# When a pick's factor is computed, and how many gather operations a double tile gets

## What is computed

```
def chunk(args):
    xc, ec, gc = args
    u = u_emb[ec]
    a = jax.nn.gelu(jnp.einsum('nd,nkd->nk', xc, u))
    return jnp.einsum('nk,nkd->nd', gc * a, v_emb[ec])
```

## Time and profile before

| | us |
|---|---|
| median of 3 runs | 4573.24 |
| lowest and highest | 4567.98, 4573.95 |
| the profiled execution | 4565.19 |
| its span | 4563.4 |
| TensorE busy (matmul) | 4388.7 |
| VectorE busy | 2760.2 |
| ScalarE busy | 1736.6 |

### The profile page before, as it was taken

One profiled execution on the slowest core, in us unless ns is written; L12 is line 12 of the kernel. 1 busy time (PEld: TensorE's weight loads), 2 busy tenths in 40 slices (PEclk: granted clock), 3 DMA queues, 4 the chain that ended last, 5 costly groups with the idle time before them and its releaser, 6 DMA issues. The chain is left out here.

```text
span 4563.4 us, 62015 instructions
## 1 busy us (share of the span) xinstructions
PE 4388.7 (96%) x21945; PEld 3670.3 (80%) x21945; DVE 2760.2 (60%) x4570; ACT 1736.6 (38%) x2923; POOL 797.8 (17%) x783
## 2 busy tenths in 40 slices
PE   8999999999999999999999998899999899999898
PEld 7888888888888887888888886787767788888787
DVE  5436556454344445555444288654779788777776
ACT  3323634332232235344332243442238444433333
POOL 0000000000000000000000000010677544444442
PEclk9999999999999999999999998999999999999999
DMA  3222220222222222211222221031224888888886
GB/s 136 92 102 92 92 75 37 74 95 98 101 93 92 102 86 90 105 43 47 93 101 93 100 87 65 19 129 56 93 102 184 311 323 334 320 312 319 309 307 253
DMA packets 93608, 634.50 MB, mean 139 GB/s; under 512 B 13344, under 2 KB 13728, under 8 KB 22752
## 3 DMA queue, kind: packets, MB, share of 16 engines
q1 hardware_dynamic: 58464, 412.95, 24.7%
q0 software_dynamic: 33792, 193.75, 11.2%
q10 hardware_dynamic: 1152, 25.17, 1.3%
HBM read 604.55 MB, written 27.26 MB: 138 GB/s over the span
## 5 line engine op out<-in xcount | busy, mean ns | idle before, releaser
L193 PE MATMUL PB<-XH,WH 128*128 128x512 f32 (+1 forms) x3288 | 1256.1, 382 | 41.6 <-DVE WL L3336 19.1
L195 PE MATMUL PB<-XH,WL 128*128 128x512 f32 (+1 forms) x3288 | 1234.6, 375 | 0.0
L194 PE MATMUL PB<-XL,WH 128*128 128x512 f32 (+1 forms) x3288 | 1233.9, 375 | 0.0
L174 DVE TENSOR_TENSOR WL<-RAW,WH 128x1024 fp32r<-128x1024 f32 x520 | 624.5, 1242 | 499.2 <-ACT WH L166 459.9
L193 PEld LDWEIGHTS PB<-XH,WH 128*128 128x128 f32 x3288 | 620.9, 189 | 160.0 <-DVE WL L3336 29.7
L195 PEld LDWEIGHTS PB<-XH,WL 128*128 128x128 f32 x3288 | 620.0, 189 | 100.5
L194 PEld LDWEIGHTS PB<-XL,WH 128*128 128x128 f32 x3288 | 621.8, 189 | 97.8 <-issue 1.9
L166 ACT ACTIVATE WH<-RAW 128x1024 fp32r<-128x1024 f32 x504 | 504.4, 1049 | 510.1 <-PE PB L195 481.9
L254 POOL TENSOR_TENSOR SQ<-SQ 128x512 f32<-128x512 f32 x49 | 72.5, 1480 | 2566.5 <-ACT SQ L236 2544.5
L193 PE MATMUL PB<-WH,WGH 128*128 128x512 f32 x768 | 307.7, 401 | 52.0 <-DVE WGL L3352 52.0
L3336 DVE TENSOR_TENSOR WL<-RAW,WH 128x1024 fp32r<-128x1024 f32 x220 | 269.4, 1224 | 126.4 <-ACT WH L3268 125.7
(11 more groups left out here) (441 smaller groups left out, 7153.8 us busy)
## 6 DMA issues: line engine op xcount, KB each, us to landing
RAW<-weights SPq DMA_DIRECT2D x381, 1024.0 KB, 4.8
gate_matrix<-STG ACTq DMA_DIRECT2D x4, 4096.0 KB, 12.1
GM<-gate_matrix POOLq DMA_DIRECT2D x128, 128.0 KB, 4.4
RAW<-weights SPq DMA_DIRECT2D x12, 512.0 KB, 3.8
gate_matrix<-STG ACTq DMA_DIRECT2D x3, 2048.0 KB, 7.2
GM<-gate_matrix POOLq DMA_DIRECT2D x128, 48.0 KB, 4.5
UV<-rows,IDX POOLq DMA_INDIRECT x160, 8.4
X<-x SPq DMA_DIRECT2D x4, 512.0 KB, 8.1
```

The source lines that it names most:

```text
L174: c.nc.vector.tensor_tensor(c.WL[p][:, cols], c.RAW[p][:, cols], c.WH[p][:, cols].bitcast(F32), ALU.subtract).then_inc(c.sem("w_split"), 1)
L193: c.nc.tensor.matmul(out, wh, xh, start=start, stop=False)
L194: c.nc.tensor.matmul(out, wh, xl, start=False, stop=False)
L195: return c.nc.tensor.matmul(out, wl, xh, start=False, stop=stop)
```

## The change

In `act_experts` a factor whose sum is not in the same step is no longer computed at the end of its step but in the next one, behind `high(x + 1, 0)`. A factor whose sum is in the same step stays at the end of the step. In `round_plan` a double tile has a room of 4 and no longer 5; a single one keeps 3. VectorE's, TensorE's and GpSimd's code is the same, but VectorE's order of dots and sums follows `round_plan`.

```diff
@@ round_plan
-    room = [0 if x + 1 == len(PLAN) else 5 if len(tile) == 2 else 3 for x, tile in enumerate(PLAN)]
+    room = [0 if x + 1 == len(PLAN) else 4 if len(tile) == 2 else 3 for x, tile in enumerate(PLAN)]
@@ act_experts
+    def pick_gains(x, summed):
+
+        for what, r in ROUND_PLAN[x]:
+            if what == "dot" and (("sum", r) in ROUND_PLAN[x]) == summed:
+                pick_gain(r)
...
         if more:
             high(x + 1, 0)
+        if x:
+            pick_gains(x - 1, False)
         if len(tile) == 1:
...
-        for what, r in ROUND_PLAN[x]:
-            if what == "dot":
-                pick_gain(r)
+        pick_gains(x, True)
```

## The result

The changed kernel takes 4490.42 us (median of 4 runs, 4485.33 to 4497.99), the kernel before beside it 4570.61 (4 runs, 4566.79 to 4573.95). The ratio is 0.9826, with a 95% interval of 0.9809 to 0.9843: 80 us or 1.7% faster. Forecast were 4525 with a range from 4502 to 4560. The profiled execution took 4491.90 us around a span of 4490.1, 73.3 us less than that of before.

The account below looks back on a forecast made before the run. TensorE, busy 908.2 of the loop's 980 us, was taken as the bound, waiting 71.1 us for VectorE. Without VectorE's 108 us of stalls, 48 us were to go: median 4573 - 48 = 4525 us, range 4502 to 4560.

Parts of the forecast that it names:

- The bound and the stalls: Expert loop: moving the factor removes 108 us of VectorE stalls, leaving it about 880 us, below TensorE's 908, which then paces.
- AG's thin cover: Gelu behind the moved factor: cover 0.1 us thin, 0 to 0.3 us on each of 94 single tiles; 10 us taken.
- I expect the waits for UV to stay about where they are, 40 to 70 us: VectorE's waits for gathered rows: fewer short-lead dots, but vanished stalls had also given rows time to land; 56.6 us before.
- The sum: Expert loop: TensorE becomes the bound; of its 71 us of waits a gain of 48 is taken, between 42 and 53.
- the best stretch of before: Old kernel's window 3774 to 3824, 48.44 us busy in 50; the whole loop at that rate gains 42 us.
- 3 to 5 us: TensorE's clock in the loop: fewer gaps bring its mean nearer 1.00, counted within the 48 us gain.
- The lower end of the range, 4502: Lower end of the 8 in 10 range: a gain near everything that TensorE waits, plus clock.
- (B), leads: Rival, chance 0.18: gathers' short leads decide, new row waits of 45 us against 108 saved; gain perhaps 20, 4553 us.
- (C), DMA full at 313 GB/s: Rival, chance 0.12: DMA engines already full, landing times grow by what is saved; within 5 us, 4570.
- (D), long landings: Rival, chance 0.05: earlier weight loads run beside gathers, long landings cost 60 us against 48 saved; slower, 4585 us.
- faster by more: Chance 0.87 that the whole kernel gets faster by more than about 9 us, 0.2% of its time.
- A: The forecast itself, chance 0.65: VectorE's stalls go and TensorE paces the loop; 4510 to 4538 us.

Follow-up runs that it names:

- order_only: The kernel after with a double tile's room back at 5, so only the factor is moved behind the rounding; 4509.95 us, ratio 0.9853 against the kernel before.
- gather_first_before: The kernel before, with GpSimd issuing a group's gathers ahead of its two gate-matrix loads; 4532.26 us, ratio 0.9904.
- both 4488: The kernel after with a room of 5 and the gathers issued ahead of the gate-matrix loads; 4488.40 us, ratio 0.9813 against the kernel before.
- room_only: The kernel before with a double tile's room of 4 instead of 5, the factor staying where it was; 4569.92 us, ratio 0.9985.
- a fill in each step: The kernel after with one VectorE fill of an unused 128x1024 tile ahead of each step's first WL; 4570.29 us, ratio 0.9998 against the kernel before.
- six fills: The kernel after with six such VectorE fills in a row in each of 17 double tiles; 4628.66 us, ratio 1.0130 against the kernel before.

## Why the prediction was wrong, step by step

*The bound and the stalls: right.* VectorE's regular stalls behind the factor are gone (105.3 us behind dots and sums, 7.1 now; 108 were counted), TensorE paces the loop, ScalarE's wait for PRODG fell from 337.4 to 137.7 us and its wait for TensorE ahead of the rounding grew from 19.9 to 95.9. The forecast that VectorE's waits for WH fall below 30 us was wrong, they are 83.6; the total was a bad sign to name, since it fills again at the second half of the tile when TensorE and the weights set the pace.

*AG's thin cover: harmless.* WG waited 0.9 us for AG in the whole loop, and I had put 10 us there.

*"I expect the waits for UV to stay about where they are, 40 to 70 us": wrong for the whole change, right for the order alone.* They are 19.6 us with both parts, 53.1 with the order alone. It takes both parts: the room alone leaves 47.1 us. With the order in place the room is worth 12 to 20 us. I had counted the leads (17 against 10) and then let the vanished stalls cancel them. They did not: from that WG to the dot, the dot's own wait aside, it is 13.1 us in the mean before and after. And where a lead stayed short, the rows came sooner. Round 101 has seven instructions and 7.1 us of work between WG and dot in either plan; its gather and its dot before, then after:

```profile
4163.20 1.62 POOL L3445 DMA_INDIRECT UV<-rows,IDX  x1 [0.30 <-issue]
4172.74 1.23 DVE L3319 SCALAR_TENSOR_TENSOR PRODG<-UV,XG 128x1024 f32<-128x1024 f32 x1 [4.22 <-DMA UV<-rows,IDX]
...
4133.41 1.00 POOL L3450 DMA_INDIRECT UV<-rows,IDX  x1 [0.30 <-issue]
4139.31 1.23 DVE L3324 SCALAR_TENSOR_TENSOR PRODG<-UV,XG 128x1024 f32<-128x1024 f32 x1
```

Before, the rows were there 9.5 us after the issue began, now within 5.9. Rounds 76 and 111 are alike, and in `order_only` these three don't wait either. What shortened these landings no run shows.

*The sum: the failed step.* It took what it called the best stretch of before as the pattern and left 23 to 27 us of TensorE's waits, where 17 are left; that term was 44 and measured 54. And it counted "3 to 5 us" for the clock, while TensorE's busy time fell by 21.2. Together these are 27 us of the 75 in the loop. The stretch still held all of the stalls, and it was no bound but a point on the way. It was not even the best; that one, in the kernel before, has 49.08 us of work in 50, part of it at the lower clock:

```profile
4024.00:4074.00 50.00, 49.08 (x246) 43.32 (x244) 40.29 (x51) 20.98 (x42) 21.59 (x21) 0.98 0.81 307
```

What TensorE needs was the bound: 2208 matmuls of 352 columns and 2304 of 512, at 0.161 and 0.229 us from start to start when the clock is full, are an estimated 883 us, 25 less than the 908 that I took for its work. A look at TensorE's rows behind its gaps would have shown it: in the kernel before, ten gaps have a start at half pace behind them, which costs 16 us beside the gaps (the excess over 0.161 and 0.229 us); in the kernel after one has, 1.4 us. That is 15 of the 21 us.

*The lower end of the range, 4502, "a gain near everything that TensorE waits, plus clock": wrong by its own words.* All of 71 and the 5 for the clock would have been 4497, still above the measured 4490: the clock's share had no bound of its own.

*The rivals.* (B), leads, is not what happened, but half of it was true: `gather_first_before` shows that leads alone were worth 42 us. (C), DMA full at 313 GB/s, is refuted: the loop now runs at 339 GB/s. The share of the DMA engines is 0.90, and up to 0.93 in the kernel with gathers first. (D), long landings, did not come: waits for rows fell. The chance of "faster by more" was added up wrong by a little: A, B and a quarter of C are 0.86, not 0.87.

What stays open: how far the gains of order and leads overlap in detail. The four corners are measured (none 4574, leads 4532, order 4510, both 4488), the course of most single rounds was not followed, and why short gathers landed sooner is not known. Of the 21.2 us of busy time 6 are not laid to slow starts. How many slow starts a kernel has is partly chance: `room_only` has TensorE waits of 66.2 us and a busy time for the same 4516 matmuls of 913.8, the kernel before 71.1 and 908.1, so some 5 us of the 21 may be an accident of the two executions. And what gap brings the lower clock was not measured by itself.

## What to carry to other kernels

An engine that computes small factors for another should do them behind the large work that the other needs next, not ahead of it, when that work waits for nothing of them: two instructions of 0.5 us in all, ahead of a 1.04 us rounding, cost 64 us over 110 steps. When two engines are nearly equally fast, the cost of a stall need not be in proportion to it: here 84 of 108 us cost nearly the whole gain, and the other 22 little or nothing. And the idle time of the engine at the bound is not the whole of what can be won, since its busy time shrinks with its gaps too; size a forecast from what its work takes at full clock.

## What the hardware showed

Nearly equal VectorE delay cost 58 us more in 17 long pieces than in 109 short ones. TensorE's busy time for the same 4516 matmuls was 885 to 926 us over the kernels of this study. On the whole it grew with TensorE's waits, though not strictly: 886.9 beside 16.9 us of them, 893.3 beside 26.7 (`order_only`), 915.8 beside 64.9 (a fill in each step), 908.1 beside 71.1 (before), 925.6 beside 111.9 (six fills). DMA moved 339 GB/s over 906 us with gathers, weights and gate matrices mixed, more than the 335 of the stretch that the prediction took as its pattern. Single slices went higher; the slices of the kernel after over 3573 to 4490, 23 us each:

```profile
GB/s 356 334 318 294 380 348 340 343 347 325 384 341 318 355 329 353 343 364 313 365 307 384 345 356 333 340 325 385 340 336 343 336 338 362 332 341 359 324 371 93
```

Five of them are above 370, so the 358 GB/s that the Trainium skill gives as HBM's limit for one core ("DMA: Bandwidth & Descriptors", Specifications) is no ceiling for a slice here; the mean of the loop stays below it.
